# Seven products for eight in 36 of the double tiles of three gate and up projections

## The reference, cut to what matters

```
D_MODEL = 1024; SEQ = 512; D_FF = 2816; D_FF_2 = 2816

# first block
h = rms_norm(x, norm_ffn_pre_g[l])
f = (jax.nn.silu(h @ w_gate[l]) * (h @ w_up[l])) @ w_down[l]
x = x + rms_norm(f, norm_ffn_post_g[l])

# second block, before and after its mixers
def swiglu(h, w_gu, w_down):
    gu = h @ w_gu
    gate, up = jnp.split(gu, 2, axis=-1)
    return (jax.nn.silu(gate) * up) @ w_down
x = x + 0.5 * swiglu(rmsnorm(x, ffn1_norm[l]), ffn1_w_gu[l], ffn1_w_down[l])
...
x = x + 0.5 * swiglu(rmsnorm(x, ffn2_norm[l]), ffn2_w_gu[l], ffn2_w_down[l])
```

## Time and profile before

| what | value |
| --- | --- |
| median of 3 runs | 1947.0 us (1946.43 to 1948.33) |
| profiled execution | 1947.51 us |
| its span | 1945.8 us |
| PE matmuls busy | 1924.7 us, 99% of the span |
| DVE, ACT, POOL busy | 999.6, 753.3, 240.1 us |
| DMA queue's packets | 30.7% of 16 engines |

### The profile page before, as it was taken

The page is one execution under the profiler, slowest core; times in us unless marked ns, Lnnn a source line. Parts: engine busy times, 40 slices in busy tenths (PEclk is TensorE's granted clock), DMA queues, the critical chain, the costliest instruction groups (busy, mean ns, idle before and its releaser), DMA issues.

```text
span 1945.8 us, 23922 instructions
## 1 busy us (share of the span) xinstructions
PE 1924.7 (99%) x9634; PEld 1564.1 (80%) x9634; DVE 999.6 (51%) x1497; ACT 753.3 (39%) x1165; POOL 240.1 (12%) x240
## 2 busy tenths in 40 slices
PE   9999999999999999999999999999999999999998
PEld 7777788878888888788888888777787788888887
DVE  6677535373334345733333367887654444333335
ACT  6344534453223233432322256665543333233224
POOL 5210001201011011010100112222010011011010
PEclk9999999999999999999999999999999999999999
DMA  6222233433333323333333232222332233333323
GB/s 174 58 65 66 59 99 103 119 98 98 98 97 98 98 85 111 97 95 96 95 96 97 81 113 66 66 66 66 87 98 65 76 97 96 95 96 96 97 59 104
DMA packets 340767, 176.32 MB, mean 91 GB/s; under 512 B 6481, under 2 KB 339378, under 8 KB 340658
## 3 DMA queue, kind: packets, MB, share of 16 engines
q1 hardware_dynamic: 340658, 174.79, 30.7%
HBM read 172.67 MB, written 2.10 MB: 90 GB/s over the span
## 4 chain that ended last, share of the span: by engine, by line
PE 93%; DVE 3%; ACT 2%; DMA 1%; issue 1%; POOL 0%; SPq 0%; ACTq 0%; DVEq 0%
PE ps L1107 28%; PE ps L1109 28%; PE ps L1111 28%; PE ps L1167 1%; PE ps L1147 1%; PE ps L1156 1%; PE ps L1252 1%; PE ps L1120 1%; PE ps L1270 1%; PE ps L1130 1%; PE ps L1181 1%; PE ps L1137 0%; DVE WL L1562 0%; DMA RAW<-in_ffn_w_down 0%; ACT WH L1313 0%
## 5 line engine op out<-in xcount | busy, mean ns | idle before, releaser
L1107 PE MATMUL ps<-HH,WH 128*128 128x512 f32 x1728 | 687.8, 398 | 1.3 <-ACT HH L1323 1.3
L1111 PE MATMUL ps<-HL,WH 128*128 128x512 f32 x1728 | 673.9, 390 | 0.8 <-DVE HL L1583 0.8
L1562 DVE TENSOR_TENSOR WL<-RAW,WH 128x1024 fp32r<-128x1024 f32 (+3 forms) x335 | 400.8, 1199 | 532.5 <-ACT WH L1313 532.0
L1109 PE MATMUL ps<-HH,WL 128*128 128x512 f32 x1728 | 673.2, 390 | 0.7 <-DVE WL L1562 0.7
L1313 ACT ACTIVATE WH<-RAW 128x1024 fp32r<-128x1024 f32 (+3 forms) x335 | 337.6, 1010 | 520.2 <-PE ps L1111 516.7
L1107 PEld LDWEIGHTS ps<-HH,WH 128*128 128x128 f32 x1728 | 324.4, 188 | 78.1 <-issue 9.7
L1109 PEld LDWEIGHTS ps<-HH,WL 128*128 128x128 f32 x1728 | 324.5, 188 | 72.1 <-issue 5.5
L1111 PEld LDWEIGHTS ps<-HL,WH 128*128 128x128 f32 x1728 | 324.3, 188 | 71.5 <-DVE HL L1583 2.1
L1107 PE MATMUL ps<-GH,WH 128*128 128x512 f32 x688 | 269.2, 391 | 0.0
L1111 PE MATMUL ps<-GL,WH 128*128 128x512 f32 x688 | 267.9, 389 | 0.0
L1109 PE MATMUL ps<-GH,WL 128*128 128x512 f32 x688 | 267.8, 389 | 0.0
(11 more groups left out here) (202 smaller groups left out, 1526.8 us busy)
## 6 DMA issues: line engine op xcount, KB each, us to landing
RAW<-in_ffn_w_gu SPq DMA_DIRECT2D x88, 512.0 KB, 3.8
RAW<-in_w_in SPq DMA_DIRECT2D x67, 512.0 KB, 3.8
RAW<-in_ffn_w_down SPq DMA_DIRECT2D x32, 512.0 KB, 4.1
RAW<-in_w_gate SPq DMA_DIRECT2D x22, 512.0 KB, 3.8
RAW<-in_w_up SPq DMA_DIRECT2D x22, 512.0 KB, 3.8
RAW<-in_w_out SPq DMA_DIRECT2D x16, 512.0 KB, 4.2
RAW<-in_mem_w_kv SPq DMA_DIRECT2D x16, 512.0 KB, 4.0
RAW<-in_w_down SPq DMA_DIRECT2D x16, 512.0 KB, 3.9
```

The lines of the kernel that those rows point to most:

```text
L1107: e.matmul(bk, wh, xh, start=k == 0, stop=False)
L1109: e.matmul(bk, wl, xh, start=False, stop=False)
L1111: last = e.matmul(bk, wh, xl, start=False, stop=k == kt - 1)
L1562: e.tensor_tensor(at.weight(n, "L"), m["RAW"][:, n % NRAW, 0:kt, :], at.weight(n, "H").bitcast(F32), ALU.subtract).then_inc(*sg.inc("lo", n))
```

## The change

In each feed-forward block six pairs of neighbouring tiles (PAIRS: third 0 tiles 5-6; third 1 tiles 0-1, 3-4, 6-7; third 2 tiles 0-1, 3-4) are computed with Strassen's scheme in Winograd's form, once for gate and once for up. A pair is a 2 x 2 block product: two halves of the input columns by two tiles of weights, and the positions in two halves of 256. Seven products, each of 4 chunks x 3 matmuls of 256 columns, replace eight. Five PSUM banks (a to e) take them; products 6 and 7 add into banks a and c when ACT has copied a (`sum_one`) and DVE has read c (`sum_two`, whose second sum is called c22). The remaining tiles stay plain: the first five, and 7, 2, 5, 2, 5.

- **Weights.** Four of the seven weight operands are sums of halves of the two raw tiles. POOL makes them (`combine_weights`, L2272, 128 x 512 each), and `split_to` puts each sum into the list as soon as its item is one of the next eight (LOOK) and the DMAs of its raw tiles have been issued. Splits of a pair's item are 512 columns wide (half a tile) in place of 1024.
- **Streaming operand.** During tiles 0 to 4 DVE makes N = X times gain times R (`normal`, two chunks a tile), POOL mixes them into four sums (`mix`, four adds of 256 columns a tile), ACT and DVE split these into NH and NL (`mix_split`). During tile 4's up matmuls `place` puts N's high and low part over HH and HL, chunk by chunk. From then on plain tiles need neither normed nor gate_r: Silu reads PSUM (`gate_plain`).
- **Order.** In tile 4, `place` and the next two splits stand in the list ahead of gate_up.
- **Constants.** NH and NL lie over the attention buffers, masks and reset pattern, so that masks are made later: by POOL in the down tiles of the last third of block 2 (LATE).

```
+PAIRS = ((5,), (0, 3, 6), (0, 3))
+LOOK = 8
+MIXED = (("b", 2), ("c", 0), ("a", "11"), ("e", 1), ("d", 3), ("a", "21"), ("c", "22"))
+LATE = ((3,), (4, 5), (6, 7), (8, 9), (10,), (), (), ())
...
     def split_to(self, n):
         while self.n_split < min(self.total, n):
...
+            for w, need in zip(known.weights[i + 1:i + 1 + LOOK], known.needs[i + 1:i + 1 + LOOK]):
+                if w[0] == "sum" and need < self.n_dma:
+                    self.combine_to(w[1], max(w[2], self.combined.get(w[1], 0)))
...
+    def mix(self, gen, c, gcol):
...
+        if c < 4:
+            self.normal(gen, c, gcol)
+            self.normal(gen, c + 4, gcol)
+            for a in range(2):
+                self.tiles.take(("mix", gen, c, a))
+            self.step("mix", gen, c)
+        if c:
+            for a in range(2):
+                self.step("mix_split", gen, c - 1, a, self.mixed_free)
...
+    def pair(self, gen, G, f, up, name, c0, pending):
+        n = self.weigh_pair(key, name, c0)
+        self.ahead(n)
+        for i, (b, op) in enumerate(MIXED):
...
+            self.step("product", gen, key, i, n + i)
...
+            elif i == 2:
...
+                self.step("sum_one", key, n)
...
+            elif i == 3:
...
+                self.step("sum_two", key, n)
...
+            elif i == 4:
+                self.step("sum_three", key, n)
...
+                if up:
+                    self.step("gate_mixed", key, 1)
...
+                    self.step("silu_mixed", key, 1)
...
+            self.ahead(n + i + 1)
...
+    def ffn(self, gen, gate, g0, up, u0, down, evac, third0, gcol):
...
+                if f in PAIRS[n]:
+                    self.pair(gen, G, f, 0, gate, g0 + c, pending)
+                    done = self.pair(gen, G, f, 1, up, u0 + c, pending)
...
+                    continue
...
                 self.step("gate_r", key, go, R)
+                if f == PLAIN - 1:
+                    self.mix(gen, f, gcol)
...
+                if f == PLAIN - 1:
+                    self.place(gen)
+                    self.ahead(len(self.weights))
-                self.step("gate_up", key, mu, bu)
+                self.step("gate_up", key, mu, bu, ("gr", key))
...
+                if f < PLAIN - 1:
+                    self.mix(gen, f, gcol)
...
+    def product(gen, key, i, n):
+        if i < 5:
+            wait_all(at.bank_free(("pr", key, b)))
+        elif i == 5:
+            g.wait_ge(*sg.at("gate_act", ("s1", key)))
+        else:
+            g.wait_ge(*sg.at("part_sum", ("c22", key)))
+        for c in range(4):
+            g.wait_ge(*sg.at("hi", n))
+            g.wait_ge(*sg.at(hi, ready))
+            e.matmul(bk, wh[:, c, :], xh, start=i < 5 and c == 0, stop=False, skip_group_check=i >= 5)
+            g.wait_ge(*sg.at("lo", n))
+            e.matmul(bk, wl[:, c, :], xh, start=False, stop=False, skip_group_check=i >= 5)
+            g.wait_ge(*sg.at(lo, ready))
+            o = e.matmul(bk, wh[:, c, :], xl, start=False, stop=c == 3, skip_group_check=i >= 5)
...
+    def combine_weights(key, j):
+        g.wait_ge(*sg.at(f"d_raw{rb % NRAW}", rb))
+        g.wait_ge(*sg.at(f"d_raw{ra % NRAW}", ra))
...
+        e.tensor_tensor(out, x, y, op).then_inc(*sg.inc("comb", (key, j)))
...
     def weight_dma(n):
-        if n >= NRAW:
-            g.wait_ge(*sg.at("lo", n - NRAW))
+        wait_all(plan.raw_done.get(n - NRAW, ()))
```

More of the change, by code:

```diff
@@ L159, in mtiles @@
         if ahead:
-            self.split_to(n + cnt + NSPL)
+            self.ahead(n + cnt)
         return [("mm", n + i) for i in range(cnt)]
@@ L413, in ffn @@
                 evac(n, mt, b, mm)
-                self.split_to(len(self.weights) + NSPL)
+                if n == 2 and gen == 2:
+                    for i in LATE[mt]:
+                        self.step("consts", i, done)
+                self.ahead(len(self.weights))
             self.gfree = (mm,)
@@ L590, in gate @@
             return gates[br, mt]
-        consts = iter(range(9))
+        consts = iter(range(2))
         def more_consts():
@@ new lines, in split, with mix_split, place @@
+        e.activation(at.weight(n, "H"), at.raw(n), ACT.Copy).then_inc(*sg.inc("hi", n))
+    def mix_split(gen, c, a, free):
+        g.wait_ge(*sg.at("mixed", (gen, c, 2 + a)))
+        wait_all(free)
+        e.activation(m["NH"][:, 2 * a:2 * a + 2, c, :], blocks(at.tile(("mix", gen, c, a)), 256), ACT.Copy).then_inc(*sg.inc("op_hi", (gen, c, a)))
+    def place(gen, c, free):
+        g.wait_ge(*sg.at("N", (gen, c)))
+        g.wait_ge(*sg.at(*free))
+        e.activation(m["HH"][:, c, :], at.tile(("N", gen, c)), ACT.Copy).then_inc(*sg.inc("xh", ("H", ("n", gen), c)))
@@ new lines, in gate_plain, with sum_one @@
+    def gate_plain(key, mm, bank):
+        tables.clear()
+        t = at.tile(("gt", key))
+        g.wait_ge(*sg.at(*mm))
+        wait_all(at.tile_free(("gt", key)))
+        e.activation(t, at.bank(bank), ACT.Silu).then_inc(*sg.inc("gate_act", key))
+    def sum_one(key, n):
+        g.wait_ge(*sg.at("mm", n + 2))
+        wait_all(at.tile_free(("u", key)))
+        e.activation(at.tile(("u", key))[:, 0:256], at.bank(("pr", key, "a"))[:, 0:256], ACT.Copy).then_inc(*sg.inc("gate_act", ("s1", key)))
@@ L1565, in split_half, with sum_four @@
+    def sum_four(key, n):
+        G_, f, up = key
+        u = at.tile(("u", key))
+        out = u if up else at.tile(("gt", (G_, f)))
+        g.wait_ge(*sg.at("mm", n + 6))
+        if not up:
+            wait_all(at.tile_free(("gt", (G_, f))))
+        e.tensor_tensor(out[:, 256:512], at.bank(("pr", key, "c"))[:, 0:256], u[:, 256:512], ALU.add).then_inc(*sg.inc("part_sum", ("c12", key)))
     def split_half(a):
```

379 lines of the change are left out of this document (312 added, 67 removed).

## The result

| | before | after |
| --- | --- | --- |
| median of the runs side by side | 1947.4 us | 1979.8 us (1979.4 to 1980.2) |
| ratio | | 1.0164, 95% interval 1.0151 to 1.0176 |
| span of the profiled execution | 1945.8 us | 1978.3 us |

A forecast was written before the change was run, and what follows sets the result against it. PE, 99% busy, was taken to bound the kernel. 1947.5 - 30.0 (PE term) + 54.3 (change-over) + 2 (pairs) = 1973.8, less 0.5 = 1973.3, put down as 1974 us; range 1951 to 2000.

The forecast's parts named there:

- PE term: PE's matmul row: 72 weight tiles removed (391.7 us), 3024 matmuls of 256 columns added (361.7 us), -30.0 us.
- Rival (c): Each product on PE starts late by 0.08 us, total 1994 us; chance 0.08.
- Pairs, +2 us: Small PE waits inside pairs, tightest at up's seventh product waiting for c22; 2 us in all, bounds 0 and 23.
- Rival (b): Pairs themselves bound by DVE with POOL (22.1 us against 20.1), on top of the change-over, total 1995 us; chance 0.14.
- Change-over, +54.3 us: Tiles 0 to 4 into each block's first pair: helper chain makes PE lose 18.1 us per block, bounds 39 and 63.
- The low clock: PE's clock falls after each hole, but products 4 to 6 wait for DVE anyway: 0, at most 2 us a block.
- The hole's form: Sign: PE idle some 14 us before the first product in each of three blocks, released by DVE's split into NL.
- the right chain: Change-over: weight sums awaiting DMAs delay gate_r, then gate_up, normals, mix splits and next weight split, once per tile; 18.1 us per block.
- Masks at nothing: POOL's later mask making (10.9 us of selects) lies under block 2's last down tiles, 33 us, and costs nothing.
- (a): The gain arrives: sums ready before gate_r asks, only PE term and small stalls stay, 1920 us; chance 0.14.
- (d): Not slower: change-over a third shorter than its low bound, 9 to 10 us a block, 1946 us; chance 0.05.

The follow-up runs named there:

- the first experiment: Changed kernel with only the weight sums of tiles 0 to 4 moved behind each tile's mix and mix splits; 1970.4 us, ratio 1.0121.
- the new order: Against the kernel with tiles 5-6 plain: normals and mix right behind gate_r, mix splits between gate_up and split_tile, in tiles 0 to 4; 1930.6 us.
- pair 6-7: Against the kernel with the new order and sums behind the mix (1952.7 us): first third's pair made of tiles 6 and 7, not 5 and 6; 1944.7 us.

## Why the prediction was right, and where it was not

- **PE term, -30.0 us.** A double pair takes 20.15 us (168 matmuls at 119.9 ns) and saves 1.59 against two plain tiles with gate and up: 18 x 1.59 = 28.6. Right, 1.4 too good. By the issue gap of the Trainium skill ("TensorE: Matmul & The Clock Gate", Back-to-back issue gap), which that section gives for an isolated matmul, it would have been 42.7; the trace disagrees, 119.9 ns for its 109. Rival (c) is out.
- **Pairs, +2 us.** Later thirds took 435.1 against 433.2 with no sums: +1.9, and what PE waited for was c22 at the seventh product (1.2 us of it). That it would be up's half was wrong: all three waits are in gate's. Rival (b) is out for this kernel. Without plain tiles the pairs are bound by their helpers, by more than (b) had, and through POOL's queue and a DMA as well.
- **Change-over, +54.3 us.** Measured 59.8 (20.7, 20.1, 19.1), inside its bounds of 39 and 63, and by the path that was forecast. In block 1 the last mix split ends at 480.5 where 478.2 was forecast. From there to the end of c22 it is 10.9 us, for 11.0 forecast, so that the seventh product starts at 491.5 and not at 489.2: the 2.3 us by which it is late were there at the last mix split.
- **The low clock, "0, at most 2 us a block".** What PE loses besides idle time, most of it in matmuls at half pace, is 5.7, 4.6 and 5.2 us, but it costs nothing on top: DVE goes from place to c22 without waiting for PE, and in each block PE still waits 0.65 us for c22. The 0 was right. Its reason was not exact: products 4 to 6 were to wait for DVE, while in block 1 the slow ones were the end of product 1, product 2 and the start of 3, products 4 and 5 did not wait, and 6 and 7 did (0.9 and 0.7 us). The slow matmuls of tile 4 in block 1 only shortened the hole behind them.
- **The hole's form.** PE was not idle for 14 us ahead of the first product, as the prediction's signs had it: it stood inside this product, chunk by chunk, 10.8 us in block 1, and 2.6 us in tile 4 for a weight split.
- **The cause.** Three gate_ups came 0.5 to 1.6 us late, and the time was forecast from the right chain. What that chain did not tell is what its links are worth. The experiments give, one after the other: 3.0 us per block for where the sums stand, 8.9 for the sums themselves, 5.0 for DVE's waits in the old order, 3.0 that no experiment removed with the pair in place. With the sums out of gate_r's way DVE's last mix split was 5.6 us earlier, though it stood 4.1 us for the split of a sum, and a slower place took part of that back. What failed, in my expectation of the first experiment, is the step from "this came last" to "this is what it costs"; I had not followed the chain a second time with the suspect at its new place.
- **Masks at nothing.** Right: the last down tiles of block 2 took 33.06 us in both kernels, and the stage behind them 434.6 against 434.7.
- **Rivals (a) and (d)** are out. Part of the gain was there to be had, but not by averages: with the new order and no first pair it was 1930.6.

What stays open: the last 3.0 us per block, with no sums and in the new order, were not taken apart (the waits are ACT's sum_one, 1.6 us in each block, and c22), and how much of the 8.9 is hold-up and how much is POOL's queue was shown for place alone (4.3 us).

## What to carry to other kernels

When a helper's round nearly equals the bound engine's (here 10.5 of 10.9 us), look at the lag with which it enters, not at its busy share: the lag shrank by only 0.4 us a tile, and 1.1 us off the round, by filling its waits or by a quieter neighbour, gave back 6 us per block. Before a wait in a chain is given a price, follow the chain again without it, and look at what the moved work meets at its new place. Time that the bound engine spends at a slow pace is no cost of its own as long as it would otherwise wait for the same helper. And a one-time change of operands costs as much as many repeats of the saving (here 19.9 us against 1.6 a pair), so it belongs where no saving step asks for its result at once.

## What the runs showed of the hardware

- Eight 512-column subtractions of DVE took 4.89 us alone and 9.91 beside POOL's sums; a POOL sum of 1.29 took 1.7. In that stretch (464.4 to 474.8, pair 6-7) the two did 4.9 and 5 x 1.29 us of work, 11.3 together, in 10.4: nearly as if on one engine.
- After the hole matmuls of 256 columns started 0.21 us apart until 484.1 (0.12 at the higher clock). The clock fell after a much shorter stand too. Behind a single wait of 2.6 us in tile 4 matmuls of 512 columns started 0.43 us apart, for 0.227 before, until 463.6. The granted clock of the stretch with this wait was 0.78 on the mean:

```profile
459.00:466.80 7.80, 6.95 (x23) 5.57 (x24) 2.69 (x4) 1.67 (x3) 5.06 (x5) 0.78 0.23 67
```
